# One-core fp32 chain of three blocks: order of work around two attentions, the Fourier gates and the embedding gate

## The reference, cut to what matters

```python
def first_block(x, ...):                 # modulated norm, then
    y_a = fourier_mix(u_f) @ w_fourier           # u_f: 512 columns, y_a: 1024
    y_b = (b_g * centred_conv3(c_g * v, w_conv)) @ w_conv_out
    z = sigmoid(gate_a) * y_a + sigmoid(gate_b) * y_b
    x = x + gate_m * (z @ w_o)
    x = x + gate_f * expert_choice_moe(...)      # 16 experts
def second_block(x, ...):                # LRU + sparse attention, conv FFN, then
    g_ple = sigmoid(rmsnorm(x, ple_norm) @ w_ple_gate)   # 1024 x 1024
    x = x + g_ple * (p @ w_ple_proj)                     # 256 x 1024
def third_block(x, ...):
    x = x + 0.5 * swiglu(rmsnorm(x), ffn1_w_gu[0], ffn1_w_down[0])   # FFN 0
    x = x + nsa_mixer(rmsnorm(x), ...)   # 16 heads of 64; three branches, @ w_out
    x = x + 0.5 * swiglu(...)                                        # FFN 1
    x = x + 0.5 * swiglu(...)                                        # FFN 2
    x = x + swa_mixer(rmsnorm(x), ...)   # 16 heads of 64, 2 key heads, window 128,
                                         # sinks in the softmax, @ w_out
    x = x + 0.5 * swiglu(...)                                        # FFN 3
    return rmsnorm(x, final_norm)
```

## Time and profile before

| | |
|---|---|
| Time, median of 3 runs (us) | 2791.7 (2787.57, 2793.91, 2791.7) |
| The profiled execution's own time (us) | 2793.43 |
| Its span in the profile (us) | 2791.6 |
| Mean granted TensorE clock | 0.896 |
| PE busy | 2459.9 us, 88% |
| DVE busy | 1289.0 us, 46% |
| ACT busy | 785.5 us, 28% |
| Bytes read from HBM | 718.17 MB |

### The profile page before, as it was taken

One profiled execution on the slowest core, in us unless ns is written; L12 is line 12 of the kernel. 1 busy time (PEld: TensorE's weight loads), 2 busy tenths in 40 slices (PEclk: granted clock), 3 DMA queues, 4 the chain that ended last, 5 costly groups with the idle time before them and its releaser, 6 DMA issues.

```text
span 2791.6 us, 35652 instructions
## 1 busy us (share of the span) xinstructions
PE 2459.9 (88%) x14622; PEld 1722.5 (62%) x14622; DVE 1289.0 (46%) x1856; ACT 785.5 (28%) x1106; POOL 22.4 (1%) x40
## 2 busy tenths in 40 slices
PE   7999877776777777779999999999989999997998
PEld 4997322211212222149899997888958888885887
DVE  2355100000000000035676776776586777776776
ACT  3342000000000000024334334434264334345432
POOL 1000000000000000000000000000000000000000
PEclk9999777777777777789999999999999999999999
DMA  8667999999999999985435555454404555541553
GB/s 322 221 247 299 397 417 416 418 418 418 419 418 416 417 418 418 418 328 190 158 121 181 181 188 188 154 196 177 141 12 151 188 180 189 188 174 61 181 181 120
DMA packets 272135, 720.75 MB, mean 258 GB/s; under 512 B 11240, under 2 KB 129016, under 8 KB 238880
## 3 DMA queue, kind: packets, MB, share of 16 engines
q1 hardware_dynamic: 270000, 708.88, 67.3%
q0 software_dynamic: 2032, 10.40, 1.0%
HBM read 718.17 MB, written 3.16 MB: 258 GB/s over the span
## 4 chain that ended last, share of the span: by engine, by line
PE 53%; issue 41%; DVE 3%; ACT 1%; DMA 1%; POOL 0%; DVEq 0%; SPq 0%; POOLq 0%; ACTq 0%
PE bank L1388 9%; PE bank L902 6%; PE bank L903 6%; PE bank L904 6%; PE bank L1389 4%; PE bank_pair L902 4%; PE bank_pair L903 4%; PE bank_pair L904 4%; PE bank L969 3%; DVE ring_r L2196 1%; PE bank L1020 1%; DVE HT L2836 0%; PE bank L1492 0%; PE bank L1508 0%; DVE small L2824 0%
## 5 line engine op out<-in xcount | busy, mean ns | idle before, releaser
L1389 PE MATMUL bank<-HT_r,ring_r 128*128 128x256 f32 x1408 | 395.0, 281 | 0.0
L2455 DVE TENSOR_TENSOR A<-bank,A 128x512 f32<-128x512 f32 x16 | 11.1, 692 | 584.2 <-PE bank L1169 584.2
L1389 PEld LDWEIGHTS bank<-HT_r,ring_r 128*128 128x128 f32 x1408 | 266.1, 189 | 0.7
L904 PE MATMUL bank<-HT_r,ring_r 128*128 128x256 f32 x904 | 256.1, 283 | 0.0
L1388 PE MATMUL bank<-HT_r,AB_r 128*128 128x512 f32 x640 | 228.2, 400 | 1.4 <-DVE HT_r L2204 1.4
L2196 DVE TENSOR_TENSOR ring_r<-ring,AB_r 128x2048 fp32r<-128x2048 f32 (+1 forms) x82 | 182.0, 2261 | 96.5 <-ACT AB_r L1733 96.5
L1388 PE MATMUL bank<-HT_r,AC_r 128*128 128x512 f32 x640 | 226.5, 398 | 0.0
L1169 PE MATMUL bank<-ring,A 128*32 128x512 f32 x768 | 147.1, 857 | 77.0 <-DMA ring<-in_w_gate_e 42.7
L2196 DVE TENSOR_TENSOR ring_r<-ring,A_r 128x2048 fp32r<-128x2048 f32 (+1 forms) x93 | 200.8, 2194 | 22.8 <-ACT A_r L1733 22.8
L904 PE MATMUL bank_pair<-A_r 128*128 128x512 f32 x488 | 191.6, 393 | 0.0
L2196 DVE TENSOR_TENSOR ring_r<-ring,AC_r 128x2048 fp32r<-128x2048 f32 x66 | 148.5, 2289 | 72.7 <-ACT AC_r L1733 72.6
(11 more groups left out here) (520 smaller groups left out, 4650.0 us busy)
## 6 DMA issues: line engine op xcount, KB each, us to landing
ring<-in_ffn_w_gu SPq DMA_DIRECT2D x88, 1024.0 KB, 6.9
ring<-in_w_up_e SPq DMA_DIRECT2D x48, 1024.0 KB, 26.6
ring<-in_w_gate_e SPq DMA_DIRECT2D x48, 1024.0 KB, 22.4
ring<-in_w_down_e SPq DMA_DIRECT2D x48, 1024.0 KB, 20.1
ring<-in_w_in SPq DMA_DIRECT2D x46, 1024.0 KB, 7.4
ring<-in_ffn_w_down SPq DMA_DIRECT2D x40, 1024.0 KB, 6.3
A<-in_w_gate_e SPq DMA_DIRECT2D x32, 1024.0 KB, 19.1
A<-in_w_up_e SPq DMA_DIRECT2D x32, 1024.0 KB, 26.6
```

The costliest lines, as they stand in the source:

```text
L904: return mm(out_, lhs[1], rhs[0], start=False, stop=stop, skip_group_check=True)
L1389: last = mm(both[:, 1, :], low, h_high[:, k, :], start=False, stop=(k == DC - 1), skip_group_check=True)
```

## The change

The products are the same as before; their order, the areas they use and the waits change.

- Fourier: DVE splits the first convolution slab (`low("conv_out", 0)`) behind the third of four gate products, instead of ahead of all four.
- Embedding product: the stage becomes `ple0` (gate half 0, work banks), `ple_proj` (the four projection products) and `ple1` (gate half 1, into `acc[t][1]`, after the norm's sums of squares have been read from there; a new semaphore `ple_gated` counts its sigmoids). The projection's load goes ahead of the second gate slab. ACT splits FFN 0's first slab between the two groups of sigmoids. DVE adds both parts of column half 0, then does its part of that slab's split, then adds half 1.
- NSA: per head, DVE weighs both branches, forms the low part, then takes both maxima. ACT splits `nsa_out`'s first slab behind the last head's three copies; the areas change. PE's `nsa_out` products wait for the heads one by one.
- SWA: scores(0) is issued inside the second query slab and scores(1) right behind it. ACT's order is q0, q1, split of `swa_out`'s slab 0, q2, exponentials(0), q3, exponentials(1). DVE does its part of that split before the ropes. The low part of the output is formed one head later. Probabilities go to p3[4..7] (areas named AC). `swa_out` waits head by head.

```diff
@@ plan
-Q_AT, Q_ROPE_AT = (0, 1, 2, 6), (3, 4, 5)
+Q_AT, Q_ROPE_AT = {"nsa_q": (0, 1, 2, 6), "swa_q": (0, 1, 2, 7)}, (3, 4, 5)
-    p.add("ple", "WW" * 2 + "WWWW", [1, 3, 7], split=2)
+    p.add("ple0", "WW", [1], split=1)
+    p.add("ple_proj", "WWWW", [3])
+    p.add("ple1", "AA", [1], split=1)
-            p.add("swa_q", "W" * 7, [1, 6], split=2)
-            p.add("swa_scores0", "A")
+            p.add("swa_q", "WWWWWWAW", [1, 7], split=2)
+            p.add("swa_scores1", "A")
-            p.add("swa_heads", "A" + "AWW" + "AWWW" * 5 + "WWW" * 2 + "W")
+            p.add("swa_heads", "AWW" + "AWWW" * 5 + "WWW" * 2 + "W")
@@ split_areas
-            a, b = (("A3", "A4"), ("A5", "A6"))[s]
+            t_["xn"] = twins["xn"][:, :, :].rearrange("p t d -> p (t d)")
+            a, b = {"nsa_out": (("xn", "A4"), ("A5", "A3")), "swa_out": (("A5", "A6"), ("A4", "xn"))}[name][s]
@@ SP
-        dense("ple", w_ple_gate, 2)
-        load("ple", 2, row_block(slot("ple", 2), w_ple_proj, 0, 2))
+        dense("ple0", w_ple_gate, 1)
+        load("ple_proj", 0, row_block(slot("ple_proj", 0), w_ple_proj, 0, 2))
+        dense("ple1", w_ple_gate, 1, 512)
@@ PE
+                    if inside and g and f == 0:
+                        inside()
...
+        pe.wait_ge(S["squares_done"], squares_upto(5))
+        w = split_slab("ple1", 0)
+        for t in range(TT):
+            ple_gate(w, t, acc[t][1], h_parts)
...
-        for m in range(8):
-            copied(pe, "nsa_heads", nsa_at(m, "out"))
-        for s in range(2):
-            to_acc3("nsa_out", s, o_high, o_low)
+        to_acc3("nsa_out", 0, o_high, o_low, ready=lambda k: copied(pe, "nsa_heads", nsa_at(k, "out")))
+        to_acc3("nsa_out", 1, o_high, o_low)
...
-        swa_scores(0)
-        copied(pe, "swa_q", Q_AT[3])
+        feature_major3("swa_q", 0, 0, h_parts)
+        feature_major3("swa_q", 2, 1, h_parts, between=lambda: turn_q("swa_q"), inside=lambda: swa_scores(0))
+        swa_scores(1)
+        copied(pe, "swa_q", Q_AT["swa_q"][3])
         rope("swa_rope3", 0, pairs(q3, 3))
-        swa_scores(1)
@@ ACT
+        high("ffn3_0_first", 0)
+        for t in range(TT):
+            filled(act, "ple1", t)
+            run(p_gate[:, 1, t, :], acc[t][1][:, :], ACT.Sigmoid, scale=rstd[:, t:t + 1]).then_inc(S["ple_gated"], 1)
...
+            else:
+                high("nsa_out", 0)
             filled(act, "nsa_heads", nsa_at(m, "out"))
             run(o_high[:, m, :], work_bank("nsa_heads", nsa_at(m, "out"))[:, 0:T], ACT.Copy).then_inc(S["o_high"], 1)
-            if m >= 6:
-                high("nsa_out", m - 6)
+        high("nsa_out", 1)
...
-        for m in range(2):
-            swa_exps(m)
+        for i in range(4):
+            if i == 3:
+                swa_exps(0)
+            copy_out("swa_q", Q_AT["swa_q"][i], q3[:, 2 * i:2 * i + 2, :].rearrange("p g t -> p (g t)"),
+                     scale=64 ** -0.5)
+            if i == 1:
+                high("swa_out", 0)
+        swa_exps(1)
...
-            if m == 6:
-                high("swa_out", 0)
@@ DVE
-        low("conv_out", 0)
...
+            if i == 2:
+                low("conv_out", 0)
...
+            if i == 1:
+                low("ffn3_0_first", 0)
...
-            for br in range(2):
-                if m:
+            if m:
+                for br in range(2):
                     nsa_weigh(m, br)
-                    if br:
-                        attention_low("nsa_heads", nsa_at(m - 1, "out"), m, m - 1)
-                    if m < 7:
+                attention_low("nsa_heads", nsa_at(m - 1, "out"), m, m - 1)
+                if m < 7:
+                    for br in range(2):
                         nsa_max(m + 1, br)
...
+        low("swa_out", 0)
         for i in range(3):
             turned_q("swa_q", i, "swa_q", Q_ROPE_AT[i])
...
-            if m:
-                attention_low("swa_heads", swa_at(m - 1, "out"), 8 + m, m - 1)
-        low("swa_out", 0)
-        attention_low("swa_heads", swa_at(7, "out"), 16, 7)
+            if m > 1:
+                attention_low("swa_heads", swa_at(m - 2, "out"), 7 + m, m - 2)
+        for m in (6, 7):
+            attention_low("swa_heads", swa_at(m, "out"), 9 + m, m)
```

More of the change, by code:

```diff
@@ L192, in swa_at @@
     if part == "scores":
-        return swa_at(m - 2, "first") if m > 1 else 0
+        return swa_at(m - 2, "first")
     if part == "out":
@@ L497, in split_areas @@
             return [(0, twins["AC"])] if s == 3 else [(0, t_["A5"])]
+        if name in ("ple0", "ple1"):
+            return [(0, twins["AB" if name == "ple0" else "AC"])]
         return ([(0, twins["AB"])], [(0, twins["AC"])], [(0, twins["A3"]), (2048, twins["A4"])])[s]
@@ L975, in feature_major, with feature_major3 @@
                     behind(2 * g + 1)
-        def feature_major3(name, b0, s, parts, n_k=DC, n_f=4, stride=512, src=None, between=None):
+        def feature_major3(name, b0, s, parts, n_k=DC, n_f=4, stride=512, src=None, between=None, inside=None):
             w = split_slab(name, s)
@@ L1463, in _, with ple_gate @@
         raw_normT(5, "norm4")
-        for h in range(2):
-            w = split_slab("ple", h)
-            for t in range(TT):
-                b = open_bank("ple", 2 * h + t)
-                for k in range(DC):
-                    parts = (fresh(5) if h + t == 0 else h_parts)(k, t * P, P)
-                    last = mm3(b[:, :], parts, w(512 * k, 512), k == 0, k == DC - 1)
-                batch(last)
-        w = slab("ple", 2)
+        def ple_gate(w, t, b, parts):
+            for k in range(DC):
+                last = mm3(b[:, :], parts(k, t * P, P), w(512 * k, 512), k == 0, k == DC - 1)
+            batch(last)
+        w = split_slab("ple0", 0)
+        for t in range(TT):
+            ple_gate(w, t, open_bank("ple0", t), fresh(5) if t == 0 else h_parts)
+        w = slab("ple_proj", 0)
         for h in range(2):
             for t in range(TT):
-                b = open_bank("ple", 4 + 2 * h + t)
+                b = open_bank("ple_proj", 2 * h + t)
                 for k in range(2):
@@ L1677, in _ @@
         swa_out(7)
-        for m in range(8):
-            copied(pe, "swa_heads", swa_at(m, "out"))
-        for s in range(2):
-            to_acc3("swa_out", s, o_high, o_low)
+        to_acc3("swa_out", 0, o_high, o_low, ready=lambda k: copied(pe, "swa_heads", swa_at(k, "out")))
+        to_acc3("swa_out", 1, o_high, o_low)
         ffn3(3, 11)
@@ L1980, in _, with ffn3 @@
         ffn_end("ffn2_end", 4, ACT.Gelu_apprx_tanh, 4 + 4 * plan.times["ffn2"])
-        high("ple", 0)
+        high("ple0", 0)
         raw_norm(5, "norm4", col("ple_norm_2", 0, 8))
-        high("ple", 1)
+        high("ple1", 0)
         act.wait_ge(S["rstd_ready"], norm_no(5))
-        for i in range(4):
-            filled(act, "ple", i)
-            frees(run(p_gate[:, i // 2, i % 2, :], work_bank("ple", i)[:, :], ACT.Sigmoid,
-                      scale=rstd[:, i % 2:i % 2 + 1]), "ple", i)
-        def ffn3(n, k, before, i):
-            filled(act, before, i)
+        for t in range(TT):
+            filled(act, "ple0", t)
+            frees(run(p_gate[:, 0, t, :], work_bank("ple0", t)[:, :], ACT.Sigmoid, scale=rstd[:, t:t + 1]), "ple0", t)
+        high("ffn3_0_first", 0)
+        for t in range(TT):
+            filled(act, "ple1", t)
+            run(p_gate[:, 1, t, :], acc[t][1][:, :], ACT.Sigmoid, scale=rstd[:, t:t + 1]).then_inc(S["ple_gated"], 1)
+        def ffn3(n, k, before=None, i=0):
             name = f"ffn3_{n}"
-            high(name + "_first", 0)
+            if before:
+                filled(act, before, i)
+                high(name + "_first", 0)
             raw_norm(k, f"ffnorm{n}", col("ffn1_norm_3" if n % 2 == 0 else "ffn2_norm_3", 8 * (n // 2), 8))
@@ L2025, in _ @@
         for i in range(4):
-            copy_out("nsa_q", Q_AT[i], q3[:, 2 * i:2 * i + 2, :].rearrange("p g t -> p (g t)"), scale=64 ** -0.5)
+            copy_out("nsa_q", Q_AT["nsa_q"][i], q3[:, 2 * i:2 * i + 2, :].rearrange("p g t -> p (g t)"), scale=64 ** -0.5)
         for i in range(2):
@@ L2083, in _ @@
         high("swa_q", 1)
-        for i in range(4):
-            copy_out("swa_q", Q_AT[i], q3[:, 2 * i:2 * i + 2, :].rearrange("p g t -> p (g t)"), scale=64 ** -0.5)
         def swa_exps(m):
@@ L2768, in _ @@
         ffn_end("ffn2_end", 4, conv_tile, 4 + 4 * plan.times["ffn2"])
-        low("ple", 0)
+        low("ple0", 0)
         add_parts(5, "ffn2_end", (5, 6), rstd)
@@ L2772, in _ @@
         mean(5)
-        low("ple", 1)
-        low("ffn3_0_first", 0)
+        low("ple1", 0)
         dve.wait_ge(S["x_new"], x_parts(6, 0))
@@ L2976, in swa_max @@
             of = lambda a: wide(a[:, two].rearrange("p (t d) -> p t d", t=1), 1, TT)
-            name, i = ("swa_heads", swa_at(m, "scores")) if m else ("swa_scores0", 0)
+            name, i = ("swa_heads", swa_at(m, "scores")) if m > 1 else (("swa_q", 6), ("swa_scores1", 0))[m]
```

35 lines of the change are left out of this document (18 added, 17 removed).

## The result

The changed kernel takes 2760.64 us (median of 4 runs, 2756.05 to 2763.39), the kernel before 2792.8 (median of 4 runs beside it). The ratio is 0.9886, 95% interval 0.9870 to 0.9903: faster by 1.1%. The forecast was 2761, range 2755 to 2773. On two further groups of runs, each on one chip, the changed kernel was timed again: 2761.66 against 2787.26 of before, ratio 0.9906 (0.9890 to 0.9921), and 2758.32 against 2787.29, ratio 0.9900 (0.9884 to 0.9917). So the gain is 26 to 32 us by the medians. The profiled pair, 2791.6 and 2760.1 us of span, differs by 31.5 us. One pair carries chance: three profiles of the changed kernel have spans of 2760.1, 2760.6 and 2753.0.

The account below looks back on a forecast made before the run. PE, busy 88% of the span, was taken to bound the kernel outside the DMA-bound experts. Terms 4.4 + 3.6 + 11.4 + 11.3 = 30.7 off 2793.4 gave 2762.7, on the median's scale 2761 us; range 2755 to 2773.

Parts of the forecast that it names:

- Fourier: First convolution slab's split behind the third gate product: 2.70 us wait gone, 1.7 of clock back, sum 4.4 us.
- Embedding product: End of the embedding stage: FFN 0 starts 2.9 us sooner, and 0.7 comes from the clock behind it, sum 3.6.
- NSA heads: NSA head loop: with both weighings together, PE's seven waits for the low part go, 4.4 us; bounds 0 and 4.4.
- NSA end: Last NSA head to nsa_out: waits of 2.17 and 1.90 go, 4.1 us; full clock behind the product gives 2.9.
- SWA heads: SWA head loop: low part a head later, period 3.96 to 3.2, 2.3 us over three periods; bounds 0 and 3.0.
- SWA end: T(5) to the SWA output product: 16.15 us becomes 7.8, a gain of 8.3; clock behind it 2.1.
- Left are DVE 5.5, PE 5.9: SWA end: work in us left on DVE and PE, used with a 1.9 handoff for the 7.8 us estimate.
- SWA front: Start of SWA: PE's rope waits about 3.5 us for ACT's q3 copy; net loss 0.2, plus 1.2 for one clock fall.
- Scores and one weighing done ahead give most of it back: SWA front: early scores and one weighing recover most of T(0)'s delay of about 1.1 us, leaving -0.2.
- Rival 1: Clock: new short waits at SWA's front and nsa_out's weights keep it at 0.50; costs 7 us, 2768; chance 0.16.
- Rivals 2 to 5: Head periods stay, 0.10; weight stream swallows Fourier gain, 0.06; waits only renamed, 0.03; NSA pairs at 0.50 clock, 0.03.
- the fifth rival: NSA head pairs: clock stays at 0.50 through them, seven pairs cost up to 45 us, 2806; chance 0.03.

Follow-up runs that it names:

- the move of one line: Changed kernel with DVE weighing SWA head pair 0 and taking pair 1's maxima before the rope of q3: 2754.46 us, ratio 0.9876; again 2756.92, ratio 0.9884.

## Why the prediction was right, and where it was not

- **Fourier, forecast 4.4.** From +0.65 to -3.70 by the product behind the convolution: 4.35. The wait is gone, the clock stayed at 1.00, and the shift went through the experts, as the medians of the part alone show. Right in mechanism and size.
- **Embedding product, forecast 2.9 and 0.7 of clock.** 2.78 in the profile pair, 2.8 with the part undone. The clock term went the other way in the profile pair: behind FFN 0's first product the changed kernel runs at 0.62 and 0.53, and its lead shrinks from 7.78 to 7.0 us before the clock is back. In the other two profiles of the same kernel the clock stays at 1.00. This term failed in part: the new order makes the fall rarer (two of nine profiles, against three of three), it does not settle it.
- **NSA heads, forecast 4.4.** Period 6.465 (25.86 / 4) instead of 7.10, by DVE's order alone, and the seven waits of 4.4 us in all are back with the old order. Right.
- **NSA end, forecast 4.1 and 2.9.** 4.5 and 2.7. Here both former waits are gone (4.1), and one whose cover the prediction called narrow has come: 0.91 us for the low weights. That the stretch gained more than 4.1 all the same comes from PE's work in it, which shrank from 8.68 to 7.36: before, the clock was down from 2086.4 on, not only from the product at 2090.86. The prediction had not counted this part, so two omissions of about 1 us cancel here.
- **SWA heads, forecast 2.3.** 2.45; period 3.15. By the lag alone.
- **SWA end, forecast 8.3 and 2.1 of clock.** 8.4 and 1.9. The size came out right, its division didn't: the step "Left are DVE 5.5, PE 5.9" laid it all on the split. The runs gave 4.7 to the split and 3.6 to the lag. That the total fits is luck in part.
- **SWA front, forecast a loss of 0.2 and 1.2.** It lost 1.9 (from -20.65 to -18.73), with T(0) 1.15 late where 1.1 was forecast and a wait of 3.66 where 3.5 was. The wait's size stood, and by luck: the reason fell, since ACT's copy of q3 holds nothing up, and "Scores and one weighing done ahead give most of it back" did not come in full. The wait is DVE's, for rope and maxima ahead of the weighing, as the move of one line showed.
- **Not forecast: steps where the change has nothing.** The largest in the table is from -7.78 to -9.98, at the NSA gates. In the kernel before the clock stood at 0.50 for some 10 us there:

```profile
1974.00:1976.00 2.00, 2.00 (x11) 2.00 (x10) 0.00 (x0) 0.00 (x0) 0.00 (x0) 0.50 1.05 294
1976.00:1984.00 8.00, 8.00 (x27) 5.93 (x27) 1.46 (x3) 3.41 (x4) 0.00 (x0) 0.50 0.46 128
```

In the changed kernel it did so for about 7 us (1968.6 to 1975.4). The Fourier part alone, which changes nothing there either, shows the same step, 2.4 us. So it is no gain of the change. Part of it does not last: by the end of the slow stretch the lead is 9.3 us, and by the first head pair's compressed branch 8.75 (2033.20 and 2024.45). There PE waited 2.69 us for DVE in the kernel before and 0.50 in the changed one, whose clock had been at 0.50 from 2016.4 to 2023.2: the slower clock filled a wait.

**The sum.** In the profile pair the stretches that the change touches gave 4.4 (Fourier) + 2.8 (embedding) + 4.4 (NSA heads) + 4.5 + 2.7 (NSA end and clock) + 2.5 (SWA heads) + 8.4 + 1.9 (SWA end and clock) - 1.9 (SWA front) = 29.7 us, where 30.7 were forecast. The clock at FFN 0 took 0.8 of it. The rest of the 31.5 us, 2.6, comes from stretches in which the change has nothing, the experts, what follows them and the NSA gates. The nearness of 2760.64 to the forecast 2761 is therefore luck in part: the later groups gave 26 and 29 us, and the misses at FFN 0's clock and the SWA front were made up by steps that are none of the change.

Rival 1 (the clock stays down) held in one place of four, in this profile, and the fall that was charged to the SWA front came. Rivals 2 to 5 fell: both periods shortened, the Fourier gain passed, the time is clear of no change, the head pairs ran at 1.00. The rule on transposes that the prediction took from the Trainium skill, "TensorE: Matmul & The Clock Gate", section "Part 4: PE-mode transpose", that full rate doesn't engage for transposes, spoke for the fifth rival. It is again not borne out: four pairs, in which over a quarter of PE's instructions are transposes, ran at 1.00 with PE busy throughout, and the transposes themselves start 0.11 us apart at 1.00 (from 2038.01) and 0.21 us apart at 0.50 (from 2516.30).

## What to carry to other kernels

In a loop over heads on three engines, put what the next step of the slow engine waits for first in the others' order, and let what is only stored for later (the low part here) lag by a turn. The first took the NSA loop to the bound of PE; the second took the SWA loop to within 0.5 us in three pairs of its engines' work. A weight split of several microseconds (3.70 us on ACT, 4.49 on DVE here) costs most where the last head's work queues behind it: here it did better behind the last head's copies (NSA) and under the queries' product (SWA). And look at the front of such a loop by itself: an engine that stands idle for one input while another is ready has its two jobs in the wrong order.
